# Other SBUF addresses for the TensorE operands of a two-block network kernel

## The reference

```python
def reference(x, ...):
    x = first_block(x, ...)          # gating + dilated attention + peer, depth 1
    return second_block(x, ...)      # 2 hybrid layers

def first_block(...):
    h = rms_norm(x, norm1_g)
    proj = h @ w_in                                     # 256x1024 @ 1024x2560
    ...                                                 # spatial gating, 8-head attention
    x = x + mix @ w_out                                 # 1024x1024
    x = x + peer(rms_norm(x, norm2_g), w_query, sub_keys, expert_u, expert_v)
    return rms_norm(x, final_norm_g)

def peer(xn, ...):                                      # top 16 of 128*128 experts, 8 heads
    q = xb @ w_query                                    # 1024x2048
    ...
    act = gelu(einsum('td,thkd->thk', xb, expert_u[e]))
    return einsum('thk,thkd->td', g * act, expert_v[e])

def hybrid_layer(...):
    proj = einsum('bsd,dn->bsn', x, w_in)               # 1024x4680
    ...                                                 # stick-breaking and top-k attention
    return layer_norm_2(ALPHA * x + mix @ w_out, ln_g, ln_b)
```

## The kernel before

| tensor | first byte | modulo 512 | step of its parts |
|---|---|---|---|
| H (all of the small tiles, the columns of activations) | 16512 | 128 | 1024 |
| cst (identity, suffix, masks) | 147584 | 128 | |
| X | 153216 | 128 | |
| XTh, XTl | 161408, 169600 | 128 | 1024 per chunk |
| ring, ringh, ringl | 180992, 193280, 205568 | 256 | 4096 per slot, 512 per block |
| Hh, Hl | 221888, 223936 | 192 | 1024 per column |

## Time and profile before

### The profile page before, as it was taken

How to read it: one execution, slowest core, us unless ns; L and a number is a source line. 1 busy time by engine, 2 the same in 40 slices (tenths; PEclk the granted TensorE clock), 3 DMA queues, 4 the chain that set the end, 5 groups by cost and what they waited for, 6 DMA issues and landing times.

```text
span 1342.7 us, 26744 instructions
## 1 busy us (share of the span) xinstructions
PE 1285.8 (96%) x9917; PEld 1228.0 (91%) x9917; DVE 729.6 (54%) x1494; ACT 676.4 (50%) x1202; POOL 667.8 (50%) x286
## 2 busy tenths in 40 slices
PE   7988999999999999999999999999999999799996
PEld 5876999898999999999999999999999987799875
DVE  2444049994056666675665666666547632346423
ACT  4555344444465555554545545545544564346552
POOL 6735768999866666664000000000047766567653
PEclk9989999999999999999999999999989999899998
DMA  5724545455544444445665565665564433434432
GB/s 208 260 87 145 179 138 181 167 172 172 186 143 142 142 139 139 139 139 186 191 197 190 191 198 189 192 198 189 188 220 147 137 126 128 153 128 149 142 118 79
DMA packets 59142, 218.59 MB, mean 163 GB/s; under 512 B 6657, under 2 KB 6697, under 8 KB 58689
## 3 DMA queue, kind: packets, MB, share of 16 engines
q1 hardware_dynamic: 56592, 206.07, 46.7%
q0 software_dynamic: 1792, 8.95, 1.8%
q10 hardware_dynamic: 688, 2.62, 0.5%
HBM read 215.50 MB, written 4.21 MB: 164 GB/s over the span
## 4 chain that ended last, share of the span: by engine, by line
PE 83%; issue 6%; POOL 6%; DVE 2%; ACT 1%; DMA 0%; POOLq 0%; DVEq 0%; ACTq 0%
PE A L503 26%; PE W L503 18%; POOL ringl L460 5%; PE A L527 5%; PE A L528 5%; PE A L532 4%; PE W L765 4%; PE A L547 4%; PE A L549 4%; PE A L554 4%; POOL ringl L424 1%; PE W L581 1%; PE W L928 1%; PE W L640 1%; PE W L899 1%
## 5 line engine op out<-in xcount | busy, mean ns | idle before, releaser
L424 POOL TENSOR_TENSOR ringl<-ring,ringh 128x1024 fp32r<-128x1024 f32 x137 | 337.4, 2476 | 188.2 <-ACT ringh L976 181.0
L460 POOL TENSOR_TENSOR ringl<-ring,ringh 128x1024 fp32r<-128x1024 f32 x126 | 320.1, 2547 | 114.1 <-ACT ringh L1136 83.7
L503 PE MATMUL W<-XTh,ringh 128*128 128x256 f32 x1024 | 295.7, 289 | 6.6 <-POOL ringl L460 6.5
L503 PE MATMUL W<-XTl,ringh 128*128 128x256 f32 x1024 | 289.9, 283 | 0.0
L503 PE MATMUL W<-XTh,ringl 128*128 128x256 f32 x1024 | 289.4, 283 | 0.0
L503 PE MATMUL A<-Hh,ringh 128*128 128x256 f32 x1024 | 282.8, 276 | 0.0
L503 PE MATMUL A<-Hl,ringh 128*128 128x256 f32 x1024 | 282.6, 276 | 0.0
L503 PE MATMUL A<-Hh,ringl 128*128 128x256 f32 x1024 | 282.6, 276 | 0.0
L976 ACT ACTIVATE ringh<-ring 128x1024 fp32r<-128x1024 f32 x135 | 142.0, 1057 | 162.4 <-PE A L532 74.2
L503 PEld LDWEIGHTS W<-XTh,ringh 128*128 128x128 f32 x1024 | 194.1, 190 | 8.0 <-issue 7.7
L1136 ACT ACTIVATE ringh<-ring 128x1024 fp32r<-128x1024 f32 x189 | 197.5, 1045 | 0.0
(11 more groups left out here) (263 smaller groups left out, 2117.6 us busy)
## 6 DMA issues: line engine op xcount, KB each, us to landing
ring<-exp_u SPq DMA_DIRECT2D x128, 512.0 KB, 3.2
ring<-exp_v SPq DMA_DIRECT2D x128, 512.0 KB, 4.1
ring<-w SPq DMA_DIRECT2D x72, 512.0 KB, 3.2
ring<-w_out SPq DMA_DIRECT2D x24, 512.0 KB, 3.3
ring<-w_in SPq DMA_DIRECT2D x20, 512.0 KB, 3.4
ring<-w_query SPq DMA_DIRECT2D x16, 512.0 KB, 3.3
skewed<-scratch POOLq DMA_DIRECT2D x1, 2048.0 KB, 11.1
H<-lng POOLq DMA_DIRECT2D x2, 1024.0 KB, 6.7
```

Source lines behind the costliest of these rows:

```text
L424: pool.tensor_tensor(ringl[:, slot, :], ring[:, slot, :], ringh[:, slot, :].bitcast(F32), ALU.subtract)\
L460: pool.tensor_tensor(ringl[:, slot, :], ring[:, slot, :], ringh[:, slot, :].bitcast(F32), ALU.subtract)\
L503: last = pe.matmul(dst, stationary[a], moving[b], start=start and n == 0, stop=stop and n == 2, skip_group_check=True)
```

## The change

The allocation alone changes. `home` now counts from the next multiple of 32, at which an allocation begins. XTh and XTl move from 128 to 192 modulo 512, Hh and Hl from 192 to 224. The ring's slots get 1036 elements each, of which the first 1024 are used, so that they lie 4144 bytes apart, and `ring`, `ringh` and `ringl` each begin at 160. No instruction is added, removed or moved on any engine; the shapes, the strides within an operand and the semaphores stay the same.

```diff
         def home(first):
-            n = (first - nc.sbuf_base) % 512
+            n = (first - (nc.sbuf_base + 31) // 32 * 32) % 512
...
-        home(128)
+        home(192)
         XTh = sb("XTh", [P, KC, T], F32R)
         XTl = sb("XTl", [P, KC, T], F32R)
...
-        home(256)
-        ring = sb("ring", [P, SLOTS, UNIT])
-        ringh = sb("ringh", [P, SLOTS, UNIT], F32R)
-        ringl = sb("ringl", [P, SLOTS, UNIT], F32R)
+        RING_AT = 160
+        home(RING_AT)
+        ring = sb("ring", [P, SLOTS, UNIT + 12])[:, :, 0:UNIT]
+        home(RING_AT)
+        ringh = sb("ringh", [P, SLOTS, UNIT + 12], F32R)[:, :, 0:UNIT]
+        home(RING_AT)
+        ringl = sb("ringl", [P, SLOTS, UNIT + 12], F32R)[:, :, 0:UNIT]
...
-        home(192)
+        home(224)
         Hh = sb("Hh", [P, 2, T], F32R)
```

## The result

The changed kernel took 1346.81 us (median of 13 runs, 1344.79 to 1349.62) beside 1344.04 us for the kernel before (median of 13, 1340.35 to 1345.76). The ratio is 1.0025 with a 95% interval of 1.0016 to 1.0035: slower by a small amount that can be told from none. The forecast was 1317 us.

A forecast was written before the change was run, and what follows sets the result against it. PE, busy 96% of the span, was taken to bound the kernel through the distance between matmul starts; -9.1 - 5.5 - 11.7 = -26.3 us took the median 1343.5 to 1317 us, with 1302 to 1364 to hold 8 in 10.

The forecast's parts named there:

- The difference between 113 and 119 ns is the placement of the two operands: 256-column products: distance -128 up and in column products, -64 down, explains the 5 to 6 ns between equal matmuls.
- Slot 2 repeats the pair 256 and 192: Products up and column products in slot 2 get the pair products down had, so 113.3 ns per matmul.
- C: Rival: address plays no part, the reused Hh explains 113 against 119, nothing changes, 1343.5 us; chance 0.10.
- Slots 0 and 1: Products up and column products at distances +32 and -16, shown by no trace, were taken at 113.3 ns; bound 126.
- Row products, -7.3 us: 912 matmuls of 512 columns, some 850 at full clock, each 8.6 ns quicker; ends 0 to -16 us, and +7.
- Products down, taken as 0: 3072 matmuls at new distances +64, +16, -32: no change taken, with ends of -5 and +19 us.
- A: The forecast's own case: distance decides and small is good, 1317 us, range 1298 to 1330; chance 0.45.
- D: Rival: positive distances are dear, losses in products down eat gains up; -1 to +28 us, middle 1357; chance 0.33.
- POOL sets the pace in parts of the stage ahead of the gates: In 18 of 66 units up, PE waits for POOL's remainders, so 8.2 us of gain shrinks to -5.5 us.
- Other engines and transfers cost 0: ACT, POOL and DVE work lies within PE's cover; 4% more transfer beats in ring slots would be hidden.
- B: Rival: only the known pair pays, slots 0 and 1 and products down stay unchanged; -7 us, 1336; chance 0.12.
- surcharge for starts off a multiple of 64: Starts at 160, 208, 224 cost a fetch each: 6 ns on two thirds of 7500 matmuls, +30 us.

The follow-up runs named there:

- down at 0: Against the kernel before: XTh and XTl at 192, Hh and Hl at 256 modulo 512, ring as before; measured 1347.82 us, ratio 1.0046.

## Why the prediction was wrong

*PE bounds the kernel, and the distance from start to start is the time.* Right. The stage table above adds up to the profiled executions, and no other engine's wait took over.

*The difference between 113 and 119 ns is the placement of the two operands.* Right, and shown by XT moved alone: 118.5 became 113.2 ns. (The argument against the results' place had a slip: `unit_cols` writes four PSUM regions in turn within a unit, not eight. Nothing rests on it now.)

*Slot 2 repeats the pair 256 and 192 and so takes 113.3 ns, "the one placement whose price the trace shows".* Here the first step failed. The price of ±64 isn't one number. The kernel before had shown one of two patterns, in a stage in which almost nothing interrupts PE and the slots are alike. With slots at three distances each unit enters from another one, and slot 2 landed at 117.8 in 35 of 43 units up. By the prediction's own sign (a slot-2 unit in 2.72 us, or else C holds) this would have spoken for C; XT moved alone shows that the sign was unsound.

*Slots 0 and 1: distances smaller than -64 are no dearer, since "the two known points fall toward zero".* This step carries most of the miss. Two points gave a line, and distance 0 lies at 120.0; slots 0 and 1 between the gates read 116.9 and 118.2, not 113.3. The terms that rested on it (and on the step before, for the third of the units in slot 2): between the gates -9.1 us forecast, -3.0 measured; ahead of them -5.5 against -1.1; the column and row products -11.7 against about -5.9 (the first and the last row of the stage table, which hold them).

*Row products, -7.3 us.* Mis-sized: 232.6 to 231.4 ns is 1.2 x 912 = -1.1 us at most. At +64 alone they reach 229.3.

*Products down, taken as 0, with +19 us as the end above.* +11.2 measured, within the bounds. It is the largest single miss of the sum. I had called this the large stake and then put the rule of small distances over it. The three new distances (+64, +16, -32) cost 3.7 ns more than -64 in its quick pattern, in the mean, and only half of the +64 units kept 113.3. The 1712 records fell between the prediction's two signs, 1767 for A and 1700 for D.

*POOL sets the pace in parts of the stage ahead of the gates.* Right. PE's waits for POOL's remainders rose from 6.5 to 7.0 us in the changed kernel. Windows of the kernel with XT alone moved, against the earlier trace rows:

```profile
233.00:262.00 29.00, 25.52 (x214) 24.72 (x213) 28.76 (x86) 11.42 (x19) 28.75 (x10) 1.00 0.46 156
295.00:325.00 30.00, 26.03 (x220) 25.25 (x220) 17.90 (x6) 12.21 (x19) 29.71 (x10) 1.00 0.48 159
```

Although most of the matmuls there start 5 ns closer together (6 of 18 units still read 117.8), PE gets through no more of them: 214 and 220 records for 213 and 220. Its waits for POOL rose from 6.5 to 7.6 us in that stage. The stage went from 198.6 to 194.5 us, half of the 1584 x 5.2 = 8.2. Not all of the rest is POOL's: 23 units in the slow pattern are 23 x 24 x 4.4 = 2.4 us. With down at 0, where only 4 of the 66 units were slow, the stage took 193.3 us. That is -5.3 for the -5.5 forecast: the term was right for the interval that it assumed.

*Other engines and transfers cost 0.* Right: exp_v transfers landed in 3.5 us after, 4.1 in the earlier trace rows, with a DMA share of 0.58. The 4% of further beats that the prediction estimated (133 for 128 in slot 0; by the same count slot 1, at 208, has 135) show nowhere: the ring's queue took 46.5% of the 16 engines' span, 46.7% before, for the same 206.07 MB.

*The rivals.* B, only the known pair pays, fell with that pair. C is refuted. D forecast the right side, with the loss in products down, but for a wrong reason. Its sign rule fails, as +16 is quicker than -16 and +48 than -48, while +96 is slow, and +64 has the same two values as -64; its surcharge for starts off a multiple of 64 is refuted. The +2.8 us lies within its -1 to +28, near the low end; as its reason fails, that is luck.

## What to carry to other kernels

- Where PE is full, count starts in a window, per stage and per buffer; two stages with the same matmul shape and different intervals point to the operands' addresses. Moving one tensor by 64 bytes gave 1.2% here.
- A rate read from a steady loop can be the rate of a pattern and not of a placement. Before it is carried over to a place where units alternate or are interrupted, look whether the entry is the same.
- An unknown between two measured points can be bounded by them; beyond them it can't. Where the best stage of a kernel is given up for unmeasured values, count the loss first: of the 14 distances in the table, 12 were dearer than the one given up.

## What the runs showed of the hardware

- The distance from start to start of 256-column float32r matmuls, each with its own weight load, depends on how far the moving operand's address lies from the stationary one's, modulo 256 bytes: 120.0 ns at 0 and 256, 116.4 to 120.1 elsewhere, and 113.3 to 114.7 or 117.8 at ±64, against 111.7 for matmuls of 8 and 16 columns. At a granted clock of 0.50, the lower level, the column products at -128 start every 212.5 ns, twice 106; no other distance was read there. That the operand's reads and the weight load's meet in one part of the memory would explain this, but no run showed the mechanism.
- A common shift of both by 32 bytes left the interval as it was ahead of the gates (407 records) and down (1767), and took it from 120.0 to 118.4 and 118.8 ns between the gates.
- At ±64 there are two steady patterns, which last for hundreds of matmuls (the first 21 units up, 504 matmuls, in one trace) and with slots alike change only where PE had waited, or run the gate products, between two units. A few ns at the entry of a unit go with the one or the other. What chooses is open.
